# A decoder block on one core: norm roots as a power on GpSimd, projection chunks ahead of the transposes of the probabilities, additions to x earlier on VectorE

## What is computed

```python
h = rms_norm(x, g_mix_norm) @ w_in            # q, keys, values, gates, zu, zv
o_attn = gates * (compressed + selected + window attention)   # 8 heads, 2 key heads
o_mix  = gelu(zu) * spatial(rms_norm(gelu(zv)))               # 8 channel groups
o = concatenate([rms_norm(o_attn, g_out[:512]), rms_norm(o_mix, g_out[512:])])
x = x + o @ w_out
x = x + square(relu(rms_norm(x, g_ffn_norm) @ w_ff1)) @ w_ff2
# rms_norm(a, g) = a * rsqrt(mean(a * a) + 1e-6) * g
```

## Time and profile before

| | us |
|---|---|
| median of 3 runs (605.21 to 607.37) | 606.34 |
| the profiled execution | 606.64 |
| its span in the profile | 604.6 |
| TensorE busy | 574.5 (95%) |
| VectorE busy | 443.5 (73%) |
| ScalarE busy | 368.8 (61%) |
| GpSimd busy | 123.5 (20%) |

### The profile page before, as it was taken

The page is one execution under the profiler, slowest core; times in us unless marked ns, Lnnn a source line. Parts: engine busy times, 40 slices in busy tenths (PEclk is TensorE's granted clock), DMA queues, the critical chain, the costliest instruction groups (busy, mean ns, idle before and its releaser), DMA issues.

```text
span 604.6 us, 9216 instructions
## 1 busy us (share of the span) xinstructions
PE 574.5 (95%) x3433; PEld 500.6 (83%) x3433; DVE 443.5 (73%) x725; ACT 368.8 (61%) x654; POOL 123.5 (20%) x198
## 2 busy tenths in 40 slices
PE   8999999999898878799999999999999999999997
PEld 7777777887676767687999999999998888888886
DVE  3799881786667776774977766548689996899774
ACT  6855552738666767765584359553498656656561
POOL 1550000002342433330131100320113123120200
PEclk9999999999989998999999999999999999999999
DMA  8833247251212101000599785996979979977862
GB/s 305 321 100 121 92 147 267 87 194 36 70 36 71 35 11 61 1 1 1 127 199 208 169 206 158 189 183 180 202 148 175 212 172 200 237 141 239 181 207 105
DMA packets 25164, 87.56 MB, mean 145 GB/s; under 512 B 3024, under 2 KB 3312, under 8 KB 25120
## 3 DMA queue, kind: packets, MB, share of 16 engines
q0 software_dynamic: 9856, 35.38, 31.7%
q1 hardware_dynamic: 15120, 51.59, 25.0%
q10 hardware_dynamic: 144, 0.00, 0.0%
HBM read 84.87 MB, written 2.10 MB: 144 GB/s over the span
## 4 chain that ended last, share of the span: by engine, by line
PE 76%; DVE 11%; issue 5%; ACT 5%; DMA 2%; SPq 1%; POOL 0%; DVEq 0%; ACTq 0%
PE ps L425 22%; PE ps L426 22%; PE ps L427 22%; DMA raw<-in_w 2%; PE ps L2049 1%; DVE xs L1545 1%; PE ps L1776 1%; ACT pt_sb L1046 1%; PE ps L2068 1%; PE ps L1919 1%; DVE ps L1491 1%; DVE w_lo_sb L1185 1%; DVE w_lo_sb L1189 1%; DVE pt_sb L1515 1%; ACT p_sb L1038 1%
## 5 line engine op out<-in xcount | busy, mean ns | idle before, releaser
L1020 ACT ACTIVATE w_hi_sb<-raw 128x1024 fp32r<-128x1024 f32 x112 | 118.6, 1060 | 114.8 <-PE ps L427 88.8
L1553 DVE TENSOR_TENSOR w_lo_sb<-raw,w_hi_sb 128x1024 fp32r<-128x1024 f32 x112 | 137.0, 1224 | 64.7 <-ACT w_hi_sb L1020 64.5
L656 POOL DMA_DIRECT2D raw<-in_w_ff x64 | 55.2, 863 | 246.8 <-DVE w_lo_sb L1553 222.6
L425 PE MATMUL ps<-w_hi_sb,ht_hi 128*128 128x512 f32 x192 | 81.9, 427 | 6.2 <-DVE xs L1545 4.0
L425 PE MATMUL ps<-w_hi_sb,a_hi 128*128 128x512 f32 x224 | 87.1, 389 | 0.0
L426 PE MATMUL ps<-w_lo_sb,a_hi 128*128 128x512 f32 x224 | 87.1, 389 | 0.0
L427 PE MATMUL ps<-w_hi_sb,a_lo 128*128 128x512 f32 x224 | 87.1, 389 | 0.0
L425 PE MATMUL ps<-ht_hi,w_hi_sb 128*128 128x256 f32 (+1 forms) x272 | 79.1, 291 | 0.0
L427 PE MATMUL ps<-ht_hi,w_lo_sb 128*128 128x256 f32 (+1 forms) x272 | 78.8, 290 | 0.0
L426 PE MATMUL ps<-ht_lo,w_hi_sb 128*128 128x256 f32 (+1 forms) x272 | 78.8, 290 | 0.0
L427 PE MATMUL ps<-w_hi_sb,ht_lo 128*128 128x512 f32 x192 | 75.5, 393 | 0.0
(11 more groups left out here) (237 smaller groups left out, 1150.1 us busy)
## 6 DMA issues: line engine op xcount, KB each, us to landing
raw<-in_w_ff POOLq DMA_DIRECT2D x64, 512.0 KB, 6.3
raw<-in_w_ff SPq DMA_DIRECT2D x48, 512.0 KB, 3.9
raw<-in_w SPq DMA_DIRECT2D x23, 512.0 KB, 4.6
xs<-in_x SPq DMA_DIRECT2D x8, 512.0 KB, 7.6
raw<-in_cmp_w SPq DMA_DIRECT2D x8, 512.0 KB, 4.3
xT<-in_xt SPq DMA_DIRECT2D x3, 512.0 KB, 9.1
raw<-in_w_c SPq DMA_DIRECT2D x4, 304.0 KB, 2.8
out_y<-xs SPq DMA_DIRECT2D x2, 512.0 KB, 3.4
```

Of the source, the lines that this page charges most:

```text
L425: pe.matmul(out, l_hi, r_hi, start=start, stop=False)
L656: pool.dma_start(raw[:, n % RAW, :], (w_ff1, w_ff2)[stage - 1][k, q], accum_op=ALU.add, max_dma_last_dim=8192).then_inc(raw_added[n % RAW] ...
L1020: act.activation(w_hi_sb[:, FS[j], :], raw[:, j, :], ACT.Copy).then_inc(w_hi, 1)
L1553: dve.tensor_tensor(w_lo_sb[:, FS[j], :], raw[:, j, :], w_hi_sb[:, FS[j], :].bitcast(F32), ALU.subtract).then_inc(w_lo, 1)
```

## The change

Four things are changed.

1. The square roots and reciprocals of both groups' norms are gone from ScalarE and VectorE. GpSimd computes mean plus epsilon with a `tensor_scalar` and raises it to the power -0.5 with a `tensor_tensor` against a tile of constants (`power`), with a wait for its own result between the two. It does so for the mixer before its first scaling, and for the attention's tiles 0, 1 and 2 between the two scalings of the pairs that begin at steps 24, 40 and 56, and for tile 3 after its last scaling. The additions wait for `o_rstd` where they waited for `n_rstd`.
2. On TensorE, the chunks c = 1 to 3 of a projection come before `probs_t` of the same step, where they came behind it. Chunk 0 stays behind `values`, and the transpose jobs stay ahead of `probs_t`.
3. On VectorE, an addition to `x` comes before `coefs` and `pt_low` of its step, where it came behind them.
4. GpSimd fills the tile of constants at the start.

```diff
+        power = sb("power", [P, NT])
...
+            pool.memset(power[:, :], -0.5).then_inc(power_made, 1)
...
+            def inverse_root(kind, t, n):
+
+                i = 0 if kind == "mix" else t + 1
+                pool.wait_ge(n_ssq, NORM[kind, t + n - 1] + 1)
+                pool.tensor_scalar(stat(rstd, kind, t, n), stat(ssq, kind, t, n), 1.0 / AW, EPS, ALU.mult, ALU.add
+                                   ).then_inc(o_mean, 1)
+                pool.wait_ge(o_mean, i + 1)
+                pool.tensor_tensor(stat(rstd, kind, t, n), stat(rstd, kind, t, n), power[:, 0:n], ALU.pow
+                                   ).then_inc(o_rstd, 1)
+
+            pool.wait_ge(power_made, 1)
+            inverse_root("mix", 0, NT)
...
+                if v in (24, 40, 56):
+                    inverse_root("attn", v // 16 - 1, 1)
+            inverse_root("attn", NT - 1, 1)
...
             norm_sum("mix", 3, t2[:, :])
-            norm_root("mix", 0, NT)
+            act.wait_ge(n_ssq, NORM["mix", NT - 1] + 1)
...
-                if s == 36:
-                    norm_root("attn", 0, 2)
-                if s == 52:
-                    norm_root("attn", 2)
...
-            norm_root("attn", 3)
...
-            norm_inv("mix", 0, NT)
...
-                    dve.wait_ge(n_rstd, NT + 1)
+                    dve.wait_ge(o_rstd, 1)
                 else:
-                    dve.wait_ge(n_rstd, NT + 2 + (0, 0, 1, 2)[t])
+                    dve.wait_ge(o_rstd, t + 2)
...
+                if k in ADD_NO:
+                    add(*k)
                 if 2 <= w <= NV and w % 2 == 0:
                     coefs(w // 2 - 1)
                 if 0 <= s < NV:
                     pt_low(s)
-                if k in ADD_NO:
-                    add(*k)
...
-                if s == 37:
-                    norm_inv("attn", 0, 2)
-                if s == 53:
-                    norm_inv("attn", 2)
...
-                if v in CHUNKS and CHUNKS[v][0] in TRANSPOSED:
+                product = CHUNKS[v] if v in CHUNKS and CHUNKS[v][0] in ADD_NO else None
+                if product and product[1] > 0:
+                    job(*product)
+                if v in CHUNKS and not product:
                     job(*CHUNKS[v])
                 if v < NV:
                     probs_t(v)
-                product = CHUNKS[v] if v in CHUNKS and CHUNKS[v][0] in ADD_NO else None
-                if product and product[1] > 0:
-                    job(*product)
                 if v >= LAG:
                     values(v - LAG)
```

More of the change, by code:

```diff
@@ L385, in hybrid_block @@
         n_ssq, n_root, n_rstd, n_rows = [sem(f"n_{k}") for k in ("ssq", "root", "rstd", "rows")]
+        power_made, o_mean, o_rstd = sem("power_made"), sem("o_mean"), sem("o_rstd")
         ht_half, ht_done = sem("ht_half"), sem("ht_done")
@@ L514, in p_parts, with stat @@
             return pt_sb[b][:, part, slice(0, t + 1) if t else slice(h // 2, h // 2 + 1), h % 2, :]
+        def stat(m, kind, t, n=1):
+            c = KINDS.index(kind) * NT + t
+            return m[:, c:c + n]
         XT_PARTS = [slice(0, NK + SEQ), slice(NK + SEQ, NK + 2 * SEQ)]
@@ L685, in x_parts @@
             return xT[:, NK + c * SEQ:NK + (c + 1) * SEQ], xT[:, c:c + 1], ht_hi[:, c, :], ht_lo[:, c, :]
-        def stat(m, kind, t, n=1):
-            c = KINDS.index(kind) * NT + t
-            return m[:, c:c + n]
         def norm_width(kind):
@@ L1594, in _ @@
             ht_lo_evac("ffn", 1, 1)
-            norm_inv("attn", 3)
             def late_difference(t):
```

## The result

| | us |
|---|---|
| changed kernel, median of 4 runs | 591.12 (590.58 to 592.38) |
| before, median of 4 runs | 606.86 (605.21 to 608.12) |
| ratio | 0.9745 (95%: 0.9715 to 0.9776) |
| profiled run, its span | 590.6, 588.8 |
| TensorE's mean granted clock, after and before | 1.000 and 0.991 |

What follows compares the result with a forecast made beforehand. The bound was TensorE's attention-loop waits, mostly for VectorE's addition freeing the shared projection bank. Removed table work 8.1 and reordering 4.95, discounted to 6.9 + 2.5 = 9.4 us, gave 606.64 - 9.4 = 597.2 us, range 591.5 to 604.8.

Steps and rivals of the forecast that it cites:

- the clock term: Attention loop after the long TensorE wait: 1.5 of 1.7 us lost to a lower clock comes back.
- rival B: Whole kernel: nothing comes through, waits return at the next `row_max`, clock falls elsewhere; 604.5 to 608.2 us, chance 0.10.
- step 55: Attention loop, 4.05 us TensorE wait for the addition behind two table loads and a root: gain 3.6 us.
- behind step 36: Attention loop, three TensorE waits left by a pair of table loads, 2.27 us in all: gain 2.2 us.
- first chunks: Projection first chunks waiting for the addition to x: moving it ahead gains 1.8 us at one, 1.6 at four others.
- step 45: Attention loop, 2.58 us wait mostly from older VectorE work: earlier addition gains 0.45 us, 2.1 stay.
- the two other transposes: Attention loop, two remaining transpose waits for the addition, 1.4 us in all: 0.8 us go.
- chunks ahead of the transposes: Attention loop on TensorE: chunks c = 1 to 3 fill waits for p or a free transpose bank, 0.3 us.
- Before the loop: Start of attention: root and its table load leave the path to the first exponentials, gain 0.8 us.
- A: Attention loop: reordering only turns waits into others through later `pt_high`, `row_max` and exponentials; 602.9 us, chance 0.19.
- C: GpSimd's second scalings at steps 25, 41 and 57: slow power, gain eaten at 5.0 us each; slower than before, chance 0.08.
- D: GpSimd before step 0's scaling: one slow first power of 8.0 us costs TensorE 4.0; 601.2 us, chance 0.05.

Runs made afterwards that it cites:

- `filler`: Kernel before with 8, 14 and 26 idle transposes ahead of TensorE's waits at steps 14, 45 and 55, no wait shortened: 603.36 us, ratio 0.9955.
- `chunks_only`: Kernel before with only projection chunks c = 1 to 3 moved ahead of the transposes of the probabilities: 611.1 us, ratio 1.0089.
- `adds_only`: Kernel before with only the additions to x moved ahead of `coefs` and `pt_low`: 595.2 us, ratio 0.983.
- `pow_filler`: Kernel before with only the roots as a power on GpSimd, plus 8 and 14 idle transposes ahead of steps 14 and 45: 598.02 us, ratio 0.9873.
- `splits_later`: Changed kernel with four of VectorE's low parts of weights one step later: 588.28 us, ratio 0.9716 to the kernel before.
- `no_chunks`: Changed kernel with the chunks back behind the transposes of the probabilities: 590.49 us, ratio 0.9745 to the kernel before.

## Why the prediction was wrong, point by point

**The failed step is the clock term:** "With the wait gone I take 1.5 of it back." Only the fall behind step 55 was counted. The windows showed 0.90 at 220 too, I quoted it, and gave it no price; 160 and 230 I didn't open. Over the loop it was 5.1 us in this profile and 6.1 on average over 31 runs, and 0.9 was left after the change. I forecast 1.3 us after the discount and it was 5.1: 3.8 of the 6.4 us that 15.8 is above 9.4 (at the 3.7 us that the line through the 31 runs gives the clock, 2.4). `filler` shows that it is a cost beside the waits. The rest of the 6.4 is 1.2 of waits, 0.4 of work, and 1.0 ahead of the loop, where the start of the kernel before was late by chance; that last part is luck of the profile and not the change. On the other chip the gain was 14.2 us, and the changed kernel's 591.74 there lies just inside the range. A falling clock ("the clock falls elsewhere") stood only in rival B, as a risk, though the profile showed just as well what there was to get back.

**The waits had the right size.** Forecast in the loop after the discount 7.4 us (4.9 for the loads, 2.5 for the reordering), measured 8.6:

| term | forecast, undiscounted | measured |
|---|---|---|
| step 55 | 3.6 | 3.5 |
| behind step 36 | 2.2 | 2.3 |
| first chunks | 3.4 | 2.6 |
| step 45 | 0.45 | 0.05 |
| the two other transposes | 0.8 | 0.05 |
| chunks ahead of the transposes | 0.3 | none that can be told |
| waits for `pt_low` | | 1.1 |
| waits for GpSimd | | -1.1 |

The discount of one half on the reordering was about right in the sum (2.7 of 4.65 measured), and that of 15% on the loads was not needed at the two steps (5.8 of 5.8).

**Before the loop** 0.8 was forecast, and the fourteen start times show no gain. What TensorE waits for there is `ht_lo`, now 1.44 us, where it was 0.40 for the scaling and 0.95 for `ht_lo`.

**The terms don't add.** I wrote that neither would pass in full, and gave the additions 4.65 beside the loads. Alone they give 11.0 us, the power 8.0, the two together 15.5. My account of the addition counted what it stands behind as `pt_low`'s own 0.42 us. What it stood behind was `pt_low`'s wait, for ScalarE and for the loads in front of it. That was in the earlier trace rows, as 1.36 us, and I used it at one chunk only.

**Chunks.** The edit to which I gave 0.3 us costs 5 by itself and nothing in company. No row of before says so; the order could have told it, since the addition then stood behind the low part of a transpose that the move delays.

**Rivals.** A didn't come, as the addition had left the line in which its first half acts; `chunks_only` shows that half. C needed 5.0 us a power, and it took 0.56, between my bounds. D: the first power, of four columns, took 1.05 us, and TensorE waited nowhere for GpSimd ahead of the first chunk. The Trainium skill, page "GPSIMD Engine Reference", section "Instruction dispatch", gives some 6 us for the first call of a freshly loaded kernel of GpSimd; the trace has no such first call, and whether the power's code had to be loaded at all no run here tells. B is refuted by the ratio.

**The signs I had named.** Seven loads in the program: yes. Step 55 under 1 us and the clock 1.00 from there: yes, 0.51. Additions under 5 us of waits: no, 5.8, for step 45 (2.53, "near 2") and 50 stayed. GpSimd not above 3.5: no, 4.2. The power isn't the reason: `adds_only`, which has none, waits 5.5 us for the scaling. TensorE reaches the transposes sooner and waits there instead.

**What stays open.** Why the clock falls behind one wait and not behind another of the same length (2.53 us at step 45 of the changed kernel, no fall; 1.90 in `pow_filler`, a fall). And why the profile of `adds_only` fell twice when three other runs of it hardly did.

## What to carry to other kernels

In an in-order queue, price a step by what the instructions ahead of it wait for, and not only by their own length: an addition with all its data ready stood behind one that waited for another engine, and moving two lines gave 11 of 606 us. Where TensorE has waits of 1 to 4 us, add up the granted clock over all windows, not only at the worst one, and count it as time to be had beside the waits, here some 0.7 to 1 us for each us of lost clock. Try two moves apart as well as together, for one cost 5 us alone and nothing with the other.

## What the runs showed of the hardware

A power (`pow`, tensor with tensor) on GpSimd takes 0.56 us for 128x1 and 1.05 us for 128x4, less than the 1.18 us that the two-input instruction of the earlier trace rows took for 128x1. In the kernel before, the lost clock is 6.1 us a run on average (31 runs, granted clock 0.985 to 0.994), and the spread of its times, 603.5 to 608.6, goes mostly with it. A held clock doesn't alone make runs repeat: five runs of `splits_later` at 0.999 and 1.000 lie within 588.18 to 588.31, but the sixth, at 0.999, is 589.70, and four runs of `no_chunks` at 1.000 lie between 590.26 and 591.36. Lost clock also came behind waits shorter than others that it didn't follow: 1.90 us in `pow_filler`, where 2.53 us in the changed kernel left it at 1.00.
